# A two-block network on one core: the forgetting attention moved ahead of the scan, and the normalisation of both attentions moved ahead of their fillers

## What is computed

```python
h = rmsnorm(x, ln1_w)
z, xbc, dt_raw, q, k, v, f_raw = split(h @ w_in)
y_ssd = ssd_group(z, xbc, dt_raw, ...)    # conv of 4 taps, silu, scan over 16 heads, * silu(z),
                                          # rmsnorm over 2 groups of 512
y_fox = fox_group(q, k, v, f_raw, ...)    # attention of 16 heads with a forgetting term:
                                          # s + cum[q] - cum[k], causal, softmax
x = x + concat([y_ssd, y_fox]) @ w_out
x = x + peer(rmsnorm(x, ln2_w), ...)      # product keys, 16384 experts, top 16 of 8 heads
out = rmsnorm(x, lnf_w)
```

## Time and profile before

| | |
|---|---|
| median of 3 runs | 3460.86 us |
| profiled execution | 3458.67 us |
| its span | 3456.9 us |
| TensorE busy | 3286.3 us, 95% |
| VectorE busy | 2072.9 us, 60% |
| ScalarE busy | 1516.0 us, 44% |
| mean granted TensorE clock | 0.975 |

### The profile page before, as it was taken

The page is one execution under the profiler, slowest core; times in us unless marked ns, Lnnn a source line. Parts: engine busy times, 40 slices in busy tenths (PEclk is TensorE's granted clock), DMA queues, the critical chain, the costliest instruction groups (busy, mean ns, idle before and its releaser), DMA issues.

```text
span 3456.9 us, 54474 instructions
## 1 busy us (share of the span) xinstructions
PE 3286.3 (95%) x21910; PEld 3041.9 (88%) x21910; DVE 2072.9 (60%) x3174; ACT 1516.0 (44%) x2095; POOL 29.1 (1%) x44
## 2 busy tenths in 40 slices
PE   7989998999999997999888999999999999999998
PEld 7878998999999997999778988888888888888886
DVE  4446977555545446675335478967676566666665
ACT  4444434444444334434224444454444444444444
POOL 0000000000000000000000000000000000000000
PEclk9989999999999998999889999999999999999999
DMA  9323543555555542434123466656666866666663
GB/s 282 125 96 138 186 163 134 177 182 182 182 182 182 194 171 83 173 126 155 61 85 135 160 206 207 210 201 228 221 215 230 310 244 243 242 240 241 240 219 139
DMA packets 108255, 638.72 MB, mean 185 GB/s; under 512 B 11616, under 2 KB 28160, under 8 KB 38960
## 3 DMA queue, kind: packets, MB, share of 16 engines
q1 hardware_dynamic: 100368, 591.44, 48.3%
q0 software_dynamic: 7472, 44.57, 3.6%
q10 hardware_dynamic: 240, 0.25, 0.0%
HBM read 597.42 MB, written 38.80 MB: 184 GB/s over the span
## 4 chain that ended last, share of the span: by engine, by line
PE 89%; DVE 6%; ACT 2%; issue 1%; DMA 1%; DVEq 0%; ACTq 0%; SPq 0%
PE bank L375 14%; PE bank L358 14%; PE bank L360 14%; PE bank L359 14%; PE bank L376 7%; PE bank L994 7%; PE bank L995 7%; PE bank L996 7%; DVE wlo L343 2%; PE bank L963 2%; PE bank L497 1%; ACT whi L337 1%; PE bank L494 1%; DMA raw<-stream 1%; PE bank L508 1%
## 5 line engine op out<-in xcount | busy, mean ns | idle before, releaser
L343 DVE TENSOR_TENSOR wlo<-raw,whi 128x1024 fp32r<-128x1024 f32 x1056 | 1288.6, 1225 | 1208.5 <-ACT whi L337 1205.5
L337 ACT CAST whi<-raw 128x1024 fp32r<-128x1024 f32 x1056 | 1104.5, 1048 | 1308.8 <-PE bank L360 783.8
L358 PE MATMUL bank<-xboth,whi 128*128 128x256 f32 x3312 | 948.9, 287 | 39.9 <-DVE xboth L1225 24.1
L359 PE MATMUL bank<-xboth,whi 128*128 128x256 f32 x3312 | 942.0, 284 | 0.0
L360 PE MATMUL bank<-xboth,wlo 128*128 128x256 f32 x3312 | 941.8, 284 | 0.0
L375 PE MATMUL bank<-xboth,whi 128*128 128x512 f32 x2048 | 727.0, 399 | 0.0
L358 PEld LDWEIGHTS bank<-xboth,whi 128*128 128x128 f32 x3312 | 641.6, 194 | 42.7 <-issue 39.7
L359 PEld LDWEIGHTS bank<-xboth,whi 128*128 128x128 f32 x3312 | 641.1, 194 | 0.7
L360 PEld LDWEIGHTS bank<-xboth,wlo 128*128 128x128 f32 x3312 | 640.7, 193 | 0.0
L376 PE MATMUL bank<-xboth,wlo 128*128 128x256 f32 x2048 | 573.1, 280 | 0.0
L375 PEld LDWEIGHTS bank<-xboth,whi 128*128 128x128 f32 x2048 | 384.7, 188 | 89.8
(11 more groups left out here) (348 smaller groups left out, 3030.8 us busy)
## 6 DMA issues: line engine op xcount, KB each, us to landing
raw<-stream SPq DMA_DIRECT2D x528, 1024.0 KB, 4.8
up_activations<-ust SPq DMA_DIRECT2D x128, 128.0 KB, 5.1
gate_matrix<-gstage POOLq DMA_DIRECT2D x8, 2048.0 KB, 14.0
gslice<-gate_matrix POOLq DMA_DIRECT2D x8, 2048.0 KB, 10.7
uin<-up_activations SPq DMA_DIRECT2D x32, 512.0 KB, 5.6
relative_band<-cband POOLq DMA_DIRECT2D x1, 3072.0 KB, 36.8
xraw<-xt SPq DMA_DIRECT2D x1, 2048.0 KB, 7.8
cbias<-relative_band POOLq DMA_DIRECT2D x1, 2048.0 KB, 20.8
```

Of the source, the lines that this page charges most:

```text
L337: nc.scalar.copy(whi[b.half][:, k, :], raw[b.raw][:, k, :]).then_inc(hi_done, 1)
L343: nc.vector.tensor_tensor(wlo[b.half][:, k, :], raw[b.raw][:, k, :], whi[b.half][:, k, :].bitcast(f32), ALU.subtract).then_inc(lo_done, 1)
L358: nc.tensor.matmul(o, whi[b.half][:, k, :], rhi[:, r, :], start=i == 0, stop=False)
L359: nc.tensor.matmul(o, whi[b.half][:, k, :], rlo[:, r, :], start=False, stop=False)
```

## The change

- `attend_dve`, which both attentions use: the normalisation of a pair becomes a function `scaled`, and that of pair c+1 is issued right after the maxima of pair c+1, ahead of the first filler of pair c.
- The order of the stream: after `dtf` come `fv`, `fk`, `fq`, `xbc`, `z`. The forgetting attention stands ahead of the scan. Its 16 fillers (two for each pair) are the 12 `xbc` blocks, with `conv2` on VectorE after the second filler, and the first 4 `z` blocks. `xpad` has 3 chunks in place of 12, used in turn.
- The scan has 12 fillers: the last 4 `z` blocks and 8 `w_out2` blocks, which now multiply the attention's half (the host lays the halves of `w_out2` out in the other order). There are 2 in its lead-in, 7 beside the head pairs 0 to 6, 3 around the norms. `f_done` is awaited ahead of the first head.
- The scan's two group norms: the square of group 0 is taken after head pair 4, its sum uses bank 4 between the last two heads, and norm steps and fillers alternate (`group_norm`, `group_square`, `group_hi`). The last eight `w_out2` blocks wait for the low part of group 1 (`norm_lo`).
- The clearing of `fq` on GpSimd and the load of the keys stand earlier. The arena's offsets differ.

```diff
-         ("merge", 96), ("w_out", 16), ("dtf", 1), ("z", 8), ("xbc", 12), ("fk", 8), ("fv", 8),
-         ("fq", 8), ("w_out2", 16), ("wq", 16), ("experts", 256)]
+         ("merge", 96), ("w_out", 16), ("dtf", 1), ("fv", 8), ("fk", 8), ("fq", 8), ("xbc", 12),
+         ("z", 8), ("w_out2", 16), ("wq", 16), ("experts", 256)]
...
 # attend_dve
-            maxima(0)
-            for c in range(WC):
+            def scaled(c):
                 for par in range(2):
                     den = small[:, 8 * par + 4:8 * par + 6]
...
+            maxima(0)
+            scaled(0)
+            for c in range(WC):
                 if c + 1 < WC:
                     maxima(c + 1)
+                    scaled(c + 1)
                 beside(c, 0)
...
 # TensorE
-            for name in ("z", "xbc"):
+            for name in ("fv", "fk"):
                 blocks(pe, pst, FIRST[name], COUNT[name], by_x)
+            wait_evacuated(pe, "fv")
+            turn_chunks("fv_turned", fv)
+            for n in range(8):
+                by_x(Block(FIRST["fq"] + n), 0, 0)
+                if n == 1:
+                    pe.wait_ge(sem("cum_ready"), 1)
+                    pe.wait_ge(sem("fvtok_ready"), 4)
...
+            wait_evacuated(pe, "fq")
+            pe.wait_ge(sem("cmask_ready"), 1)
...
+            def beside_f(c, i):
+                by_x(Block(FIRST["xbc"] + 2 * c + i), 0, 0)
+            attend_pe(pe, "f", fq, fk, lambda c: c, lambda j, c: fvtok[:, j, 128 * c:128 * c + 128], fprob, fprobT,
+                      forgetting, beside_f)
...
+                for n in range(first, end):
+                    if n < 4:
+                        by_x(Block(FIRST["z"] + 4 + n), 0, 0)
+                    else:
+                        by_half(Block(FIRST["w_out2"] + n - 4), 1)
+            beside_ssd(0, 1)
+            pe.wait_ge(sem("att_exp"), 4 * HEADS)
+            pe.wait_ge(sem("att_o"), 2 * HEADS)
             pe.wait_ge(sem("xconv_ready"), 1)
             turn_chunks("xs_turned", xconv)
-            beside_ssd(1, 3)
+            beside_ssd(1, 2)
...
+            pe.wait_ge(sem("f_done"), 1)
             for h in range(HEADS):
-                if h % 2 == 0:
-                    beside_ssd(3 + h // 2, 4 + h // 2)
+                if h % 2 == 0 and h < 14:
+                    beside_ssd(2 + h // 2, 3 + h // 2)
...
+                if h == 14:
+                    norm_sumsq(pe, "s0", ssq, 4)
...
-            for g in range(2):
-                beside_ssd(11 + 2 * g, 13 + 2 * g)
-                norm_pe(pe, f"s{g}", None, ssq, 4, None, centre=False)
-            beside_ssd(15, 16)
...
+            beside_ssd(9, 10)
+            norm_sumsq(pe, "s1", ssq, 4)
+            beside_ssd(10, 12)
             for n in range(8, 18):
                 if n < 16:
-                    by_half(Block(FIRST["w_out2"] + n), 1)
+                    pe.wait_ge(sem("norm_lo"), turn("lo", "s1"))
+                    by_half(Block(FIRST["w_out2"] + n), 0)
...
 # VectorE
+            def beside_f(c, i):
+                lo_only(Block(FIRST["xbc"] + 2 * c + i), 0, 0)
+                if i == 1 and c < 6:
+                    conv2(2 * c)
+                    conv2(2 * c + 1)
...
+            dve.wait_ge(sem("f_hi"), 1)
+            nc.vector.tensor_tensor(mlo[:, 8:16, :], fo[:, :, :], mhi[:, 8:16, :].bitcast(f32),
+                                    ALU.subtract).then_inc(sem("f_done"), 1)
...
+            group_norm(0, 0)
+            group_norm(0, 1)
+            beside_ssd(9, 10)
+            group_norm(1, 0)
+            beside_ssd(10, 11)
+            group_norm(1, 1)
+            beside_ssd(11, 12)
...
 # ScalarE
+                if c == 4:
+                    group_square(0)
+            norm_sqrt(act, "s0", sst)
+            group_hi(0)
+            beside_ssd(9, 10)
+            group_square(1)
+            norm_sqrt(act, "s1", sst)
+            beside_ssd(10, 11)
+            group_hi(1)
+            beside_ssd(11, 12)
```

More of the change, by code:

```diff
@@ L225, in build @@
     st16 = [ar(f"st16_{i}", [128, T], 96 + i) for i in range(5)]
[L227 to L230, removed]
+    zg = ar("zg", [128, WC, T], 64)
+    xpad = ar("xpad", [128, XPAD, T + CONV2_K - 1], 28)
+    xconv = ar("xconv", [128, 12, T], 16)
+    xtok = ar("xtok", [128, NT, 1024], 0)
     dtfs = ar("dtfs", [128, T], 96)
@@ L692, in _ @@
                                     ).then_inc(sem("cb_masked"), 1)
[L694 to L698, removed]
+            pool.wait_ge(sem("norm_lo"), turn("lo", "s1"))
             pool.dma_start(pk[:, :, :].rearrange("p k n -> p (k n)"), keys).then_inc(sem("keys_loaded"), 16)
@@ L848, in turn_chunks @@
                     ins.then_inc(sem(name), 1)
-            pe.wait_ge(sem("cumT_ready"), 1)
+            wait_evacuated(pe, "fv")
[5 more added lines that the diff above has]
+                    pe.wait_ge(sem("fvtok_ready"), 4)
+                    for i, src in enumerate((cum, dtfs)):
+                        for j in range(NT):
+                            ins = nc.tensor.transpose(bank(6)[:, 256 * i + 128 * j:256 * i + 128 * j + 128],
+                                                      src[:, 128 * j:128 * j + 128], ident[:, :])
+                    ins.then_inc(sem("cum_turned"), 1)
@@ new lines, in beside_f, with by_half, beside_ssd @@
+            def beside_f(c, i):
+                by_x(Block(FIRST["xbc"] + 2 * c + i), 0, 0)
+            attend_pe(pe, "f", fq, fk, lambda c: c, lambda j, c: fvtok[:, j, 128 * c:128 * c + 128], fprob, fprobT,
+                      forgetting, beside_f)
+            def by_half(b, part):
+                for h in range(2):
+                    product(pe, b, mhi, mlo, ks=range(8 * h, 8 * h + 8), k0=8 * part, cols=T * h, first=h == 0,
+                            last=h == 1)
+            def beside_ssd(first, end):
+                for n in range(first, end):
[3 more added lines that the diff above has]
+                        by_half(Block(FIRST["w_out2"] + n - 4), 1)
@@ L1280, in _ @@
-            blocks(dve, st, FIRST["xbc"], COUNT["xbc"], conv2, per_turn=4 * CONV2_K)
-            dve.sem_inc(sem("conv2_done"), 1)
+            for name in ("fv", "fk"):
+                blocks(dve, st, FIRST[name], COUNT[name], lo_only)
+            for n in range(8):
+                lo_only(Block(FIRST["fq"] + n), 0, 0)
+                if n == 0:
+                    for r in range(4):
+                        dve.wait_ge(sem("fv_turned"), r + 1)
+                        nc.vector.tensor_copy(
+                            fvtok[:, :, 256 * r:256 * r + 256].rearrange("p j (h d) -> p h j d", h=2),
+                            bank(4 + r)[:, :].rearrange("p (h j d) -> p h j d", h=2, j=NT)
+                        ).then_inc(sem("fvtok_ready"), 1)
+                if n == 2:
+                    dve.wait_ge(sem("cum_turned"), 1)
+                    nc.vector.tensor_copy(cumT[:, :, :], bank(6)[:, 0:256])
+                    nc.vector.tensor_copy(dtT[:, :, :], bank(6)[:, 256:512]).then_inc(sem("cumT_ready"), 1)
@@ new lines, in conv2 @@
+            def conv2(c):
+                b = Block(FIRST["xbc"] + c)
+                dve.wait_ge(evacuated[b.bank], b.uses())
+                acc, src = xconv[:, c, :], xpad[:, c % XPAD, :]
+                for k in range(CONV2_K):
+                    w = vcol("conv2_w", c * CONV2_K + k)
+                    if k == 0:
+                        nc.vector.tensor_scalar(acc, src[:, 0:T], w, vcol("conv2_b", c), ALU.mult, ALU.add
+                                                ).then_inc(sem("conv2_tap"), 1)
+                    else:
+                        dve.wait_ge(sem("conv2_tap"), CONV2_K * c + k)
+                        nc.vector.scalar_tensor_tensor(acc, src[:, k:k + T], w, acc, ALU.mult, ALU.add
+                                                       ).then_inc(sem("conv2_tap"), 1)
@@ new lines, in beside_f, with add_x1_pair @@
+            def beside_f(c, i):
+                if c == 0 and i == 0:
+                    dve.wait_ge(sem("xpad_ready"), 1)
+                lo_only(Block(FIRST["xbc"] + 2 * c + i), 0, 0)
+                if i == 1 and c < 6:
+                    conv2(2 * c)
+                    conv2(2 * c + 1)
+            attend_dve(dve, st, "f", fprob, fsmall, fo, None, False, beside_f)
+            def add_x1_pair(b, i, g):
+                lo_only(b, i, g)
+                dve.wait_ge(mm_done, b.count(1))
+                j = (b.n0 - FIRST["w_out2"]) % 8
+                dst = x1[:, 2 * j:2 * j + 2, :]
+                nc.vector.tensor_tensor(dst, dst, bank(b.bank)[:, :].rearrange("p (a n) -> p a n", a=2), ALU.add
+                                        ).then_inc(evacuated[b.bank], 1)
@@ L1290, in _ @@
-            dve.wait_ge(sem("cumT_ready"), 1)
             for r in range(4):
@@ L1331, in _ @@
                     st.link(nc.vector.tensor_tensor(yy, yy, zg[p0:p1, c, :], ALU.mult))
[L1332 to L1338, removed]
@@ L1698, in _, with to_xpad @@
```

(34 more changed lines are left out.)

163 lines of the change are left out of this document (51 added, 112 removed).

## The result

The changed kernel takes 3373.07 us (median of 4 runs, 3371.92 to 3378.13) against 3460.82 us (median of 4): 87.8 us less, ratio 0.9749 with a 95% interval of 0.9738 to 0.9761. The forecast was 3383 with a range of 3366 to 3412. The profiled execution took 3371.92 us, its span is 3370.2 us, the mean granted clock 0.986 (0.975 before).

What follows compares the result with a forecast made beforehand. TensorE, busy 95%, was taken as the bound, losing time to idle gaps and half clock in both attentions. From 3458.7 us, 39 and 39 off gave 3380.7; 2.2 for the median made 3383 us, range 3366 to 3412 (own range 3366 to 3399).

Steps and rivals of the forecast that it cites:

- First attention: First attention: normalisation ahead of the fillers ends the wait of the transposes; pair period 22.0 to 16.3 us, gain 39 us.
- the forecast's second count: First attention: gain counted as 24.5 us of idle plus 15 of half-speed time, 39.5 us, beside 40 by pair periods.
- Forgetting attention to the last `w_out2` blocks: Stretch from z's first block to the last eight `w_out2` blocks: 454.3 us becomes 413; gain taken as 39, bounds 30 to 46.
- the four new waits: TensorE waits: `f_done` 3.0 us, last scan pair's matrix 4.8, group 1's square 6.2, second norm's low part 1.8.
- The timeline sum: Same stretch, term by term: 402.8 us of work and waits, about 10 for the clock after five idle spots, 413 together.
- two ways of counting: Same stretch: gain 41 us by the sum of terms, 38 by idle and clock alone; 39 taken.
- the step from the profiled execution to the median: Whole kernel: the runs' median is 2.2 us above the profiled execution, turning 3380.7 into 3383 us.
- Rival A: Both attentions: clock doesn't recover, half-speed spots stay and only idle goes; 3410 us, chance 0.08.
- Rival B: Scaling ahead holds splits back, or scan rounds pass 7.93 us and the tail is 10 longer; 3400 to 3412, chance 0.17.
- Rival C: Both attentions: VectorE's queue becomes the chain if splits are only one block ahead; slower, 3500 us, chance 0.03.
- Rival D: First (c) attention gains nothing, since GLU products and table loads take the gap's place; 3422 us, chance 0.05.
- The conversion of table switches: ScalarE: about six added switches, 16 us at the skill's price, 8 by the row without drain; both beside TensorE work.

## Why the prediction was right

*First attention, 39 us forecast, 41.3 measured.* The pair's period was forecast at 16.3 us and is 16.13. By the forecast's second count idle time was to give 24.5 us and gave 24, and the clock was to give 15 and gave 17: it kept more half-speed time for the opening than there was. The first pair's wait stayed, as said.

*Forgetting attention to the last `w_out2` blocks, 39 forecast, 45.5 measured.* By terms: the four new waits were forecast at 3.0, 4.8, 6.2 and 1.8 us and measure 3.3, 4.6, 5.9 and 1.6. The pairs were to take 18.3 us; from the second transposes (1470.81) to the last (1580.77) they take 18.33 each. The scan's full pairs take 7.93, as said. The timeline sum was 403 us of work and waits and 10 for the clock. From 1299.3 (the first block, 41.3 earlier than before) to the first of the last eight blocks is 409.7:

```profile
1709.01 0.39 PE L359 MATMUL bank<-mhi,whi 128*128 128x256 f32 x1 [1.60 <-DVE mlo L1250]
```

The sum without the clock was 402.8, so if it holds, the term that was mis-sized is the clock: 7 us and not 10. The windows above agree: 0.01 of 157, 0.09 of 20 and 0.12 of 41 us below full speed are some 16 us at 1.2 GHz, at most 8 us lost. Another 2 us are a choice: two ways of counting gave 41 and 38, and 39 was taken. About 1 us more comes behind 1709: the first 10 us of the last eight blocks run at clock 1.00 now and ran at 0.80 before, behind the gap of 6.8 us.

*Both together* are 86.8 us against 78: every step was of the forecast sign. The result is 10 us below the forecast. One of them is no part of the change: 2.2 us were added for the step from the profiled execution to the median, and here it is 1.2. Of the other 8.8 us some 6 are clock that came back beyond what was forecast (2 in the first attention, 3 in the second stretch, 1 behind it). What a gap costs shows in the first attention's period, 22.0 before and 16.1 now: a wait of 3.2 to 3.6 us cost 5.9.

*Rival A (the clock stays down)* is out: 0.97 and 0.99, and the filled gap shows that idle time, not the mix of matmuls, set it. In the scan's full pairs fillers of 5.8 us and small matmuls of 2.2 us in other banks take turns, without idle time (48.00 of 48 us busy), and the clock is 1.00. With the gaps filled the first attention has short idle spots in each pair, of 0.3 to 0.7 us, and the clock is 1.00 there too. The Trainium skill ("TensorE: Matmul & The Clock Gate", section "A second HAM failure mode: psum-queue depth-cycling") describes a kernel in which short idle times between groups, with PSUM banks used in turn, make the clock oscillate; here that is so for gaps of 2.07 us (the normalisation alone, clock 0.72 behind most of them) and not for those of 0.3 to 0.7 us.

*Rival B (half the place taken by new waits)* is out as a size: the four waits were in the sum already. Its mechanism, VectorE near its limit in the scan, is real, as 1.2 us more per pair showed.

*Rival C (slower, VectorE's queue becomes the chain)* did not happen in this kernel, but a slower kernel was near: with the normalisation behind the convolutions the same order takes 3472.67 us. There the awaited step stands behind other work; a version with splits only one block ahead, the rival's own condition, was not tried.

*Rival D (nothing in the first attention)* is out: 41.3 us.

*The conversion of table switches:* six were expected in addition, it was one (9 before and 10 now from `dtf` to the norm), and taking four away changed nothing, so what a switch costs can't be read from the times. The time line of ScalarE shows it; in the changed kernel:

```profile
1620.77 1.04 ACT L338 CAST whi<-raw 128x1024 fp32r<-128x1024 f32 x1 [1.78 <-PE bank L361]
1621.84 1.28 ACT L1602 ACT_TABLE_LOAD   x1
1623.13 0.39 ACT L1602 ACTIVATE zg<-bank 128x256 f32<-128x256 f32 x1
1623.54 1.28 ACT L1776 ACT_TABLE_LOAD   x1
```

The loads follow the operations ahead of them by 0.02 to 0.03 us, and the activation follows its load by 0.01. So the 1.28 us of the load that the Trainium skill gives ("ScalarE: Activation LUTs", section "What ACT_TABLE_LOAD costs") are there, and its drain of 1.38 us is on neither side; the measurement decides, as it did in the earlier trace rows.

*One term was too high and cost nothing:* a convolution takes 1.9 us and not 2.4.

## What to carry to other kernels

When the bound engine waits at the end of each round, write down for the helper engine what stands ahead of the awaited step and whether that work's own input comes late. Here a 1 us normalisation stood behind a split whose input came from the last matmul of the round, and moving it up gave 53 of 88 us. Then ask what is awaited next: with one filler it was the output copy, and with two it was no longer waited for; and a longer queue of helper work is safe only once the awaited step no longer stands behind it. Where gaps drop the TensorE clock, price a gap above its length, here by some 70%.

## What the runs showed of the hardware

In the first attention a gap of 3.2 to 3.6 us in each pair from the second on, repeated every 22 us, was followed by a stretch at 1.2 GHz each time; with 13 useless matmuls in seven of the eight gaps the clock over the first attention rose from 0.88 to 0.97 (1.00 in the filled part) and the kernel became 10.7 us faster. With the normalisation alone moved, gaps of 2.07 us in the forgetting attention were followed by such a stretch in six of seven cases; two of the seven, where the gap ends at 1662.05 and at 1678.70:

```profile
1662.00:1668.00 6.00, 5.95 (x31) 0.72 0.55 178
...
1678.00:1684.00 6.00, 5.30 (x36) 1.00 0.50 179
```

Idle spots of 0.3 to 0.7 us, two in each pair of the filled version, were followed by none.

Chained VectorE operations on 256 columns (L1302, L1306) ran with some 0.03 us between them (four in 1.9 us). In the kernel before the same four stand in a loop, with their semaphore targets and their offsets held in registers, and had 0.18 us between them; which of the two makes the gap was not tested.
